# Gate and up projections by seven block products in place of eight, neighbouring tile pairs interleaved

## The reference

```python
def swiglu(h, w_gate, w_up, w_down):
    return (jax.nn.silu(h @ w_gate) * (h @ w_up)) @ w_down

x = x + 0.5 * mx[:, 2] * swiglu(modulate(rms_norm(x), mx[:, 0], mx[:, 1]), w_ffn_gate[l, 0], w_ffn_up[l, 0], w_ffn_down[l, 0])
# D_MODEL = 1024, D_FF = 2816, DEPTH = 2; the context stream xc uses the same weights with its own modulation
```

## Time and profile before

| what | value |
|---|---|
| time, median of 3 runs | 2960.72 us (2960.25 to 2960.83) |
| the profiled execution, its own time | 2958.43 us |
| its span, first to last instruction | 2956.6 us |
| mean granted TensorE clock | 0.991 |
| TensorE matmuls busy | 2862.2 us, 97%, 16509 matmuls |
| VectorE, ScalarE, GpSimd busy | 1489.7, 949.4, 269.6 us |
| HBM read | 255 MB, 87 GB/s over the span |

### The profile page before, as it was taken

How to read it: one execution, slowest core, us unless ns; L and a number is a source line. 1 busy time by engine, 2 the same in 40 slices (tenths; PEclk the granted TensorE clock), 3 DMA queues, 4 the chain that set the end, 5 groups by cost and what they waited for, 6 DMA issues and landing times. The chain is left out here.

```text
span 2956.6 us, 42812 instructions
## 1 busy us (share of the span) xinstructions
PE 2862.2 (97%) x16509; PEld 2681.2 (91%) x16509; DVE 1489.7 (50%) x2301; ACT 949.4 (32%) x1523; POOL 269.6 (9%) x272
## 2 busy tenths in 40 slices
PE   8999999999988899999999999999999989999999
PEld 4999999989978789999999899999998978888887
DVE  5554355454477745543554555245345577633332
ACT  3221122133368732211221322111224378532222
POOL 1000000022213310000000100000003224100000
PEclk9999999999999999999999999999999999999999
DMA  5333234222100223332342243233223201323333
GB/s 204 121 114 118 81 121 135 85 62 58 49 13 8 68 74 118 114 104 81 121 134 72 74 135 126 63 111 109 70 59 90 56 13 34 91 85 102 90 98 94
DMA packets 364164, 263.00 MB, mean 89 GB/s; under 512 B 11086, under 2 KB 339188, under 8 KB 364048
## 3 DMA queue, kind: packets, MB, share of 16 engines
q1 hardware_dynamic: 360976, 256.86, 28.8%
q10 hardware_dynamic: 2432, 4.46, 0.4%
q0 software_dynamic: 640, 0.09, 0.0%
HBM read 255.08 MB, written 2.10 MB: 87 GB/s over the span
## 5 line engine op out<-in xcount | busy, mean ns | idle before, releaser
L425 PE MATMUL pair<-h_lo,w_hi 128*128 128x384 f32 (+1 forms) x2656 | 911.9, 343 | 3.4 <-DVE w_lo L399 3.4
L426 PE MATMUL pair<-h_hi,w_hi 128*128 128x384 f32 (+1 forms) x2656 | 911.8, 343 | 0.0
L427 PE MATMUL pair<-h_hi,w_lo 128*128 128x384 f32 (+1 forms) x2656 | 911.1, 343 | 0.0
L425 PEld LDWEIGHTS pair<-h_lo,w_hi 128*128 128x128 f32 x2656 | 499.4, 188 | 25.0 <-issue 3.6
L427 PEld LDWEIGHTS pair<-h_hi,w_lo 128*128 128x128 f32 x2656 | 499.1, 188 | 21.2
L426 PEld LDWEIGHTS pair<-h_hi,w_hi 128*128 128x128 f32 x2656 | 499.4, 188 | 20.8
L399 DVE TENSOR_TENSOR w_lo<-w_raw,w_hi 128x1024 fp32r<-128x1024 f32 (+1 forms) x262 | 349.4, 1334 | 326.2 <-ACT w_hi L392 323.0
L392 ACT ACTIVATE w_hi<-w_raw 128x1024 fp32r<-128x1024 f32 (+1 forms) x267 | 301.2, 1128 | 538.9 <-PE pair L427 512.8
L425 PE MATMUL pair<-s_lo,w_hi 128*128 128x384 f32 (+1 forms) x1100 | 377.7, 343 | 0.0
L427 PE MATMUL pair<-s_hi,w_lo 128*128 128x384 f32 (+1 forms) x1100 | 377.2, 343 | 0.0
L426 PE MATMUL pair<-s_hi,w_hi 128*128 128x384 f32 (+1 forms) x1100 | 377.1, 343 | 0.0
(11 more groups left out here) (258 smaller groups left out, 3712.7 us busy)
## 6 DMA issues: line engine op xcount, KB each, us to landing
mod_raw<-in_w_mod_rows SPq DMA_DIRECT2D x64, 1024.0 KB, 4.8
w_raw<-in_w_ffn_gate SPq DMA_DIRECT2D x88, 512.0 KB, 3.8
w_raw<-in_w_ffn_up SPq DMA_DIRECT2D x88, 512.0 KB, 3.8
w_raw<-in_w_ffn_down SPq DMA_DIRECT2D x64, 704.0 KB, 4.5
w_raw<-in_w_in SPq DMA_DIRECT2D x32, 512.0 KB, 4.0
w_raw<-in_w_out SPq DMA_DIRECT2D x12, 512.0 KB, 3.6
w_raw<-in_w_q_up SPq DMA_DIRECT2D x8, 576.0 KB, 4.1
mod_first<-in_w_mod ACTq DMA_DIRECT2D x4, 1024.0 KB, 14.5
```

Of the source, the lines that this page charges most:

```text
L425: eng.matmul(dst, wh, rl, start=first, stop=False)
L426: eng.matmul(dst, wh, rh, start=False, stop=False)
L427: last = eng.matmul(dst, wl, rh, start=False, stop=end)
```

## The change

Gate and up of two neighbouring feature tiles (256 features) are one block product of 2 x 2: the 1024 input features in two halves of 4 chunks, the feature pair in two tiles, the tokens in two halves (384 columns, 256 in the last block). The seven products are those of Winograd's form of Strassen's method. A product `(u, x)` of unit u (even: gate, odd: up of pair u // 2) is an operation of 4 chunks x 3 matmuls. `p1` and `p2` take the first token half as it is (`a_hi_t`, `a_lo_t`) and plain weight blocks. The others take the sums `s1` to `s4` of the normed tokens or the second half's lower chunks (`a22`), which `ff_open_act`, `ff_open_dve` and `ff_open_pool` make once per block, and for four of them weight differences `t1` to `t4`, which GpSimd makes for every unit (`ff_t`). Results go through three PSUM chains per unit and VectorE adds them into the four result blocks (`ff_event`: `u2`, `a`, `c22`, `c21`, `c12`, and `c11` for up units).

More of the change, by code:

```diff
@@ L124 @@
 for _l in range(DEPTH):
[L125 to L136, removed]
+    MIX_T0.append(len(WIDTHS))
@@ new lines, in ff_sequence @@
+def ff_sequence():
+    seq = []
+    for p, n in enumerate(FF_PARTS):
+        first, last = 2 * FF_FIRST[p], 2 * (FF_FIRST[p] + n) - 1
+        at = {}
+        for u in range(first, last + 1):
+            for x, offset in OFFSET.items():
+                at[u, x] = 7 * u + offset
+        at[first + 1, "p1"] -= 2.5
+        at[last - 1, "p4"] += 2.5
+        part = sorted((op for op in at if op not in OPENING), key=lambda op: at[op])
+        seq += (OPENING if p == 0 else []) + part
+        seq += [("d", p, d) for d in range(KD)]
+    return seq
@@ L618, in part_products @@
-        def part_products(eng, o, chunks, lhs, rhs, a, b, before=None, done=None):
-            for k in range(chunks):
-                if before:
-                    before(k)
-                part_product(eng, o, k, lhs, rhs, a, b, k == 0, k == chunks - 1, done)
-        def part_product(eng, o, k, lhs, rhs, a, b, first, end, done):
-            (wh, wl), (rh, rl), dst = lhs(k), rhs(k, a, b), pair[o.odd][:, a:b]
-            eng.matmul(dst, wh, rh, start=first, stop=False)
-            eng.matmul(dst, wh, rl, start=False, stop=False)
-            last = eng.matmul(dst, wl, rh, start=False, stop=end)
-            if end and done is not None:
-                last.then_inc(done, 1)
@@ L669, in open_pe, with cross_pool, mix_open_pe @@
+        def cross_pool(eng, q):
+            n = len(tail_tiles(q))
+            for e in range(n):
+                if e < n - 1:
+                    tail_add(eng, q, 1, e)
+                for k in chunks_by(q, e):
+                    norm_lo_pool(eng, q, 0, k)
+        def mix_open_pe(eng, q, tiles, cols):
+            at, inst, parts = chunks_at(q), norms[q]["after"], norm_parts(q)
             for k in range(KD + LAG):
@@ new lines, in wait_s, with down_chunk @@
+        def wait_s(eng, inst, p, c):
+            done = inst * FF_PAIRS + FF_FIRST[p] + c // 2 + 1
+            for piece in (2,) if c % 2 else (0, 1):
+                eng.wait_ge(s_lo_done[piece], done)
+        def down_chunk(eng, inst, i, c, blocks, first, end):
+            wh, wl = stationary(inst, i)(c)
+            for a, b, x in blocks:
+                eng.matmul(x[:, 0:b - a], wh, s_hi[:, c, a:b], start=first, stop=False)
+                eng.matmul(x[:, 0:b - a], wh, s_lo[:, c, a:b], start=False, stop=False)
+            for a, b, x in blocks:
+                last = eng.matmul(x[:, 0:b - a], wl, s_hi[:, c, a:b], start=False, stop=end)
+            return last
@@ new lines, in ff_sp, with snapshot @@
+            for h in range(2 if pairs else 0):
+                mod_load(eng, pairs[0], h)
+            n = 2
+            for i in range(N_OPS):
+                while n < len(RAWS) and RAW_LAST[n - 2] - LO_LEAD <= i:
+                    ff_load(eng, inst, n)
+                    n += 1
+                for v, k in MOD_STEPS[inst].get(i, ()):
+                    if k % 2 and v + 1 in pairs:
+                        mod_load(eng, v + 1, k // 2)
+            first_loads(eng, following)
+        def snapshot(eng, inst, u):
+            eng.wait_ge(f_used, op_count(inst, POS[u, "p1"]))
+            if u >= 2:
+                eng.wait_ge(f_event, event_count(inst, u - 2, "c21"))
+            eng.activation(snap[u % 2][:, 0:half_of(inst)], chain(inst, u, 0), ACT.Copy).then_inc(f_snap, 1)
```

1411 lines of the change are left out of this document (957 added, 454 removed), and 4 rows, old and new, of the table FF_SEGS.

## The result

The changed kernel takes 3093.0 us (median of 4 runs, 3091.1 to 3094.2) against 2960.5: ratio 1.045, 95% interval 1.0432 to 1.0468. The prediction, 2930 and faster, was wrong, and so was its range. The profiled execution took 3091.8 us, with a span of 3089.9 against 2956.6, 133.3 longer.

A forecast was written before the change was run, and what follows sets the result against it. The prediction took TensorE's matmul columns as the bound: 2956.6 - 155.2 + 67 + 8 + 45 + 5 = 2926.4 us span, 2930 as time. Its own range was 2900 to 2950 (chance 0.42), eight in ten 2845 to 3015.

The forecast's parts named there:

- What goes: Feed-forward gate and up units: 84 matmuls replace 96, saving 137.3 us in three blocks and 17.9 in the last, 155.2 together.
- Rival 4: Products cost more than the pitch in their new order, 10 ns on each of some 7,400: 74 us, 3004; chance 0.03.
- rival 2: Units with dots: GpSimd and VectorE's two-SBUF-input operations share one line, 18.2 us against 14.56; 2993, at worst 3050; chance 0.26.
- the sizing of the units: Gate and up units: overruns of the shared line sum to 115 us, leads absorb some; 45 taken, bounds 15 and 115.
- rival 3: Last block alone turns bad: 12.7 us in line against 10.08 per unit, 58 instead of 8 or so; 2980; chance 0.07.
- The test named in advance: TensorE gaps in parts with dots would show the shared line; equal times with and without dots would rule out the lock.
- Openings: Start of each feed-forward block: stalls while sums of normed tokens are made, plus late reciprocals; 67 us, bounds 46 and 95.
- The clock: Lower clock after a pause of some length: 2 us for each of four openings, 8 in all, bounds 0 and 12.
- Part ends: Down products wait for the last pair's low parts, about 6 us where 6.2 are allowed; 24 ends at 0 to 1: 5.
- Crossings: Where blocks meet: TensorE waits some 5 us for the sum of squares, today idles 3.3; cost 0, bounds -6 and +15.
- The residuals and the loads: Down operations hide the residuals, 3.5 us in 4.16; loads cost nothing, up to 10 us in the last block.

The follow-up runs named there:

- short dots: Changed kernel with the modulation dots over 8 of 1024 columns, other products left out: 2993.0 us, ratio 1.0099 to 1.0133 to the kernel before.
- short differences: Changed kernel with GpSimd's weight differences of units 2 to 21 over 2 of every 128 columns: 2943.2 us, ratio 0.9929 to 0.9962 to the kernel before.
- the PSUM operand: Changed kernel with the modulation dots' second operand read from PSUM instead of SBUF, still 1024 columns: 3015.3 us.
- the best: Changed kernel with ScalarE and low parts reordered, openings rewritten, and low parts of s before those of weights at part ends: 2948.1 us.
- ScalarE's order: Changed kernel with ScalarE's copies, Silu and roundings after a product put ahead of rounding the next weights: 3036.1 us.

## Why the prediction was wrong

**What goes: right.** 155.2 predicted, 155.5 in the trace, and the pitch of 256 columns is 0.1200 in the new order too, where the estimate from the Trainium skill (TensorE: Matmul & The Clock Gate, "Back-to-back issue gap") was 98 ns. Rival 4 falls.

**What bounds it after: the shared line, rival 2.** In the three blocks with dots its mechanism is shown from both sides (short dots, short differences) and by itself (the PSUM operand). It gave 2993 and at the worst 3050; the kernel took 3093. Beyond that worst case lies the clock: 65 us where it allows 12.

**The step that failed is the sizing of the units**, "Not all of it stops TensorE", 45 of 15 to 115. The units idle for 119 us and lose about 36 more to the clock, 155: more than the whole overrun. Block by block, block 3's 46.5 idle and 15 of clock are 62, about what rival 3 gave for it (2.6 x 22 = 57); in the other three 72.9 and 20 stand against overruns of 95. The lead gave back nearly nothing. I compared an overrun with the lead as lengths, 8.3 us of low parts. But the queue with that lead also carries the sums, with a lead of two operations, and they wait behind whatever is late in it: p3's wait for such a sum is 82.4 of the 119. The prediction named the lag of two operations under rival 2 and didn't use it in the sum. In block 3 the work done ahead under the down products gave nothing back either: a part of two pairs ran 10 us over and not 4.

The test named in advance holds: parts of two pairs with dots idle for about 5 us in blocks 1 and 2 (7.6, 5.1, 5.0 and 6.0 in block 1), the last part of each, which has none, for 0.4. In block 1 that last part took 58.6 us against 58.2 by the pitches.

**Openings**, 67 (46 to 95): 94 idle, at the upper end. The contention was in the sum; a snapshot behind a table load and two roundings was not, nor the load that waits for the last low part. But the sum also added 67 to a span in which the openings already idled for about 29, which it didn't take off. What the change added is 65, so the term came out right by luck: two errors cancel.

**The clock**, 8 (0 to 12): 65. I priced four openings. They lose 23 us to it, about 14 more than before. Stalls of 3 to 5 us come in the units at every second pair, and the clock drops there, too: the units lose about 36 us, the part ends 8. It was low for 270 us in all. That it is a consequence of the idle time is argued, not shown by an experiment of its own. Over three kernels the two fall together (idle 418, 354, 303 us in all and low clock 270, 218, 161, for the changed kernel, the one with low parts on VectorE and the best), but not in step: with ScalarE's order it is 385 and 203.

**Part ends**, 5 (24 at 0 to 1): 33, about four us of them at each one-pair part of the first three blocks, which has no older chunk to begin with. Each end was priced by a chain on free engines, not by the queue in which its last link stands; the kernel with the ends reordered shows it, 30 to 17.

**Crossings**, 0 (-6 to +15): where blocks meet TensorE idles for about 18 us before and 17 after, inside the bounds. The residuals and the loads cost nothing that TensorE waits for in the down products (1.3 us in all).

In sum 125 us of cost were predicted in these terms and 286 came, 161 more. The units with their clock are 110 of that. The chance of 0.26 for rival 2 was too small: its line of 18.2 us against 14.56 in every unit with dots should have made it the likeliest.

## What to carry to other kernels

When an engine's slack pays for a change, count what hides behind that slack today: 256 dots that cost nothing before cost 100 us after, and 29 once the queues were in a better order. Where VectorE and GpSimd both read two operands from SBUF, add their times into one line, and give an overrun of that line its full price unless every consumer in the queue, not just the one with the longest lead, can be late. The repair left out no work: serve what TensorE waits for first on each queue, and move work with a short lead off the slower engine of the line. This brought the seven-product kernel from 3093 to 2948, 0.4% below the eight-product one. And when stalls are added to a measured span, take off those that it already holds.

## What the runs showed of the hardware

A two-input instruction on VectorE is held while one on GpSimd runs (1.29 us at 512 columns): dots of 1.23 us took up to 2.33, and none over 1.23 with one operand in PSUM. GpSimd is held the same way (in the kernel with short differences, those of 0.2 us each had a median of 0.52 in the form t4, which reads an earlier difference and mostly comes behind a low part of VectorE). Matmuls of 384 columns at the lower clock start 0.32 us apart against 0.1733, 1.85 times as long.
